# Weight matrices stored as column blocks in a one-core hybrid diffusion layer: each row of a load 4 KB long instead of eight pieces of 512 bytes

## The reference

```python
hx = modulate(rms_norm(x, norm1_w), sh1, sc1)            # shifts and scales from c @ w_mod
hc = modulate(rms_norm(ctx, norm1_w), csh1, csc1)
rx, rgx, qx, kx, vx, gax, gbx = split_cols(hx @ w_in)    # w_in: 1024 x 5632
rc, _, _, kc, vc, _, _        = split_cols(hc @ w_in)
# (A) RG-LRU in both directions over conv(rx), started from the context's last states
y_r = (h_f + h_b) * gelu(rgx)
# (B) windowed attention, 8 heads of 128, 2 key heads, window 128, context keys, a sink per head
y_a = windowed_attention(rope(qx), rope(kx), vx, kc, vc, sink)
y = sigmoid(gax) * (y_r @ w_o_rnn) + sigmoid(gbx) * (y_a @ w_o_attn)
x = x + g1 * (y @ w_out)
hx2 = modulate(rms_norm(x, norm2_w), sh2, sc2)
a, v = split(dwconv(hx2 @ w_up, 3 taps))                 # w_up: 1024 x 6144
x = x + g2 * ((gelu(a) * v) @ w_down)                    # w_down: 3072 x 1024
return rms_norm(x, final_norm_w)
```

## Time and profile before

| | us |
|---|---|
| median of 3 runs | 1898.85 |
| lowest, highest | 1897.75, 1898.92 |
| the profiled execution | 1898.04 |
| its span | 1896.3 |
| busy in the span: TensorE | 1776.7 |
| VectorE | 1223.6 |
| ScalarE | 714.8 |
| GpSimd | 591.6 |

### The profile page before, as it was taken

One profiled execution on the slowest core, in us unless ns is written; L12 is line 12 of the kernel. 1 busy time (PEld: TensorE's weight loads), 2 busy tenths in 40 slices (PEclk: granted clock), 3 DMA queues, 4 the chain that ended last, 5 costly groups with the idle time before them and its releaser, 6 DMA issues.

```text
span 1896.3 us, 23019 instructions
## 1 busy us (share of the span) xinstructions
PE 1776.7 (94%) x8276; PEld 1466.8 (77%) x8276; DVE 1223.6 (65%) x1355; ACT 714.8 (38%) x919; POOL 591.6 (31%) x276
## 2 busy tenths in 40 slices
PE   3998899999899979999998798999999999999997
PEld 1887688888688768878886675888888888888886
DVE  5873667768513777775114679999998988525423
ACT  5433666557200157771002014544444444302202
POOL 2125777676344745534452680000000000000000
PEclk8999899999899979999999899999999999999999
DMA  9124112111245300005223661232222223622212
GB/s 365 49 89 122 42 48 67 59 58 45 87 135 177 77 12 1 0 27 170 81 66 135 236 199 39 89 96 81 88 77 88 77 88 119 230 100 85 99 44 90
DMA packets 184525, 182.11 MB, mean 96 GB/s; under 512 B 10512, under 2 KB 162448, under 8 KB 182288
## 3 DMA queue, kind: packets, MB, share of 16 engines
q1 hardware_dynamic: 176784, 148.26, 24.3%
q10 hardware_dynamic: 7680, 33.04, 5.2%
HBM read 145.09 MB, written 30.93 MB: 93 GB/s over the span
## 4 chain that ended last, share of the span: by engine, by line
PE 69%; DVE 16%; DMA 4%; issue 4%; ACT 3%; POOL 3%; ACTq 1%; SPq 0%; DVEq 0%; POOLq 0%
PE acc L840 14%; PE acc L841 13%; PE acc L842 13%; PE gp L840 9%; PE gp L842 9%; PE gp L841 9%; DVE pt_lo L2095 2%; DVE smax L2065 2%; DMA wst<-in_w_out 2%; DMA qs<-qf 1%; DVE wgr L2131 1%; DVE yq L2048 1%; POOL wlo_both L687 1%; PE acc L875 1%; POOL whi_both L685 1%
## 5 line engine op out<-in xcount | busy, mean ns | idle before, releaser
L840 PE MATMUL acc<-hx_hi,whi_both 128*128 128x512 f32 x672 | 265.6, 395 | 43.2 <-POOL wlo_both L687 23.0
L841 PE MATMUL acc<-hx_lo,whi_both 128*128 128x512 f32 x672 | 264.6, 394 | 0.0
L842 PE MATMUL acc<-hx_hi,wlo_both 128*128 128x512 f32 x672 | 263.9, 393 | 0.0
L685 POOL TENSOR_TENSOR whi_both<-wst,ones 128x1024 fp32r<-128x1024 f32 x63 | 169.1, 2683 | 286.0 <-PE acc L842 203.2
L687 POOL TENSOR_TENSOR wlo_both<-wst,whi_both 128x1024 fp32r<-128x1024 f32 x63 | 189.0, 2999 | 4.9
L840 PEld LDWEIGHTS acc<-hx_hi,whi_both 128*128 128x128 f32 x672 | 128.1, 191 | 71.8 <-POOL wlo_both L687 23.7
L842 PEld LDWEIGHTS acc<-hx_hi,wlo_both 128*128 128x128 f32 x672 | 128.0, 190 | 27.2
L841 PEld LDWEIGHTS acc<-hx_lo,whi_both 128*128 128x128 f32 x672 | 128.2, 191 | 25.9
L840 PE MATMUL acc<-T_hi,fac_hi 128*128 128x512 f32 x264 | 102.8, 389 | 0.3 <-DVE fac_lo L2289 0.3
L842 PE MATMUL acc<-T_hi,fac_lo 128*128 128x512 f32 x264 | 102.7, 389 | 0.0
L841 PE MATMUL acc<-T_lo,fac_hi 128*128 128x512 f32 x264 | 102.7, 389 | 0.0
(11 more groups left out here) (335 smaller groups left out, 4782.6 us busy)
## 6 DMA issues: line engine op xcount, KB each, us to landing
wst<-in_w_in SPq DMA_DIRECT2D x50, 512.0 KB, 3.9
wst<-in_w_up SPq DMA_DIRECT2D x26, 512.0 KB, 4.6
wgr<-in_mod_rest ACTq DMA_DIRECT2D x6, 2048.0 KB, 10.5
ffn_row_scratch<-ca SPq DMA_DIRECT2D x24, 512.0 KB, 2.6
wst<-in_w_down SPq DMA_DIRECT2D x32, 384.0 KB, 3.3
g_in<-ffn_row_scratch SPq DMA_DIRECT2D x24, 512.0 KB, 6.4
wup<-in_w_up SPq DMA_DIRECT2D x22, 512.0 KB, 4.9
wmod<-in_mod_first SPq DMA_DIRECT2D x8, 1024.0 KB, 11.6
```

The lines of the kernel that those rows point to most:

```text
L685: nc.gpsimd.tensor_tensor(whi[s][:, 0:kc, :], wst[s][:, 0:kc, :], ones_of(kc), mult).then_inc(S["w_hi"], 1)
L840: mm(out_ap, w_h, x_h, start=first, stop=False)
L841: mm(out_ap, w_h, x_l, start=False, stop=False)
L842: return mm(out_ap, w_l, x_h, start=False, stop=last)
```

## The change

Each weight matrix is given to the kernel in another order. The host copies the matrix into blocks of 128 columns, and within a block puts first the partition, then the eight chunks of rows, then the columns. A block is then 512 KB in one piece, and the 4 KB that belong to a partition are contiguous. `w_down` is cut also into its four pieces of 768 rows, so a row of a load is 3 KB. In the kernel only the source address patterns change; a block is now picked by its number. Sizes, order, queues and waits of the loads stay. Each of SP's loads `wst<-in_w_in 128x8x128` becomes `wst<-in_w_in 128x1024`, and in loops six register instructions on SP ahead of other loads and stores are no longer emitted.

```diff
-            w_in = D["w_in"][0].rearrange("(k p) n -> p k n", p=P)
-            w_or = D["w_o_rnn"][0].rearrange("(k p) n -> p k n", p=P)
-            w_oa = D["w_o_attn"][0].rearrange("(k p) n -> p k n", p=P)
-            w_out = D["w_out"][0].rearrange("(k p) n -> p k n", p=P)
-            w_up = D["w_up"][0].rearrange("(k p) n -> p k n", p=P)
-            w_dn = D["w_down"][0].rearrange("(k p) n -> p k n", p=P)
+            w_in, w_or, w_oa, w_out, w_up = (D[n] for n in ("w_in", "w_o_rnn", "w_o_attn", "w_out", "w_up"))
+            w_dn = D["w_down"]
 
             def col(w, base, i):
-                return w[:, :, ds(base + i * P, P)] if not isinstance(i, int) else w[:, :, base + i * P:base + i * P + P]
+                if isinstance(i, int):
+                    return w[base // P + i]
+                return w.rearrange("b p k n -> p b k n")[:, ds(i + base // P, 1), :, :].rearrange("p o k n -> p (o k) n")
...
-                sp.dma_start(wst[n % 2][:, 0:PK, :], w_dn[:, PK * q:PK * (q + 1), P * m:P * (m + 1)]).then_inc(dn_loaded[n % 2], 16)
+                sp.dma_start(wst[n % 2][:, 0:PK, :], w_dn[q, m]).then_inc(dn_loaded[n % 2], 16)
...
+def by_column_block(w):
+
+    w = np.asarray(w)[0]
+    return np.ascontiguousarray(w.reshape(KC, P, -1, P).transpose(2, 1, 0, 3))
+
+
+def by_piece(w):
+
+    return np.ascontiguousarray(np.asarray(w)[0].reshape(PIECES, PK, P, KC, P).transpose(0, 3, 2, 1, 4))
...
+    arrays.update({n: by_column_block(inputs[n]) for n in ("w_in", "w_o_rnn", "w_o_attn", "w_out", "w_up")})
+    arrays["w_down"] = by_piece(inputs["w_down"])
```

## The result

| | before | changed |
|---|---|---|
| median of 6 runs each, us | 1897.41 | 1882.55 |
| lowest, highest | 1896.27, 1898.92 | 1877.26, 1886.70 |
| the profiled execution | 1898.04 | 1886.70 |
| its span | 1896.3 | 1884.9 |
| its mean granted clock | 0.973 | 0.976 |

The ratio is 0.9925, with a 95% interval from 0.9905 to 0.9945: 14.9 us less by the medians, 17.9 were predicted, and the range 1872 to 1890 holds it. But no execution took 1882.55 us. Three took 1877.3 to 1879.5, three 1885.6 to 1886.7, and the median is the middle between the two groups. The profiled execution is of the upper one, and there the gain is 11.3 us.

The account below looks back on a forecast made before the run. TensorE, busy 94% of the span, was taken as the bound nearly everywhere. Terms 1.6 + 6.3 + 10.0 = 17.9 us off 1898.04 gave 1880.1, plus 0.8 for the median of runs: 1881.0 us, range 1872 to 1890.

Parts of the forecast that it names:

- Stage of w_out, -10.0: Stage of `w_out`: block 1 lands with the first `wgr` group, TensorE restarts at 1045.1; 10.0 us less, floor 5, ceiling 18.
- equal turns by packets: Stage of `w_out`: each of 16 engines takes one packet from each queue in turn, so block 1 needs 8 turns, not 64.
- no new wait: Stage of `w_out`: block 2 lands at about 1051 and is split by 1057, so TensorE gets no new wait.
- Rival (d): Stage of `w_out`: VectorE becomes the bound, its sums slowed beside GpSimd; stage +5.1 us, total 1903.5 us; chance 0.03.
- Rival (c): Stage of `w_out`: block 1 is through ahead of the first group and the clock stays up; 1872.9 us; chance 0.12.
- Before attention, -6.3: Query stage before attention: both long swaps of query halves shorten; 6.3 us less, floor 0, ceiling 6.8.
- Without that both swaps take 2.31 us: Before attention: once the weight load no longer holds them, the 6.07 and 5.34 us swaps shorten, saving 3.76 + 3.03 = 6.8.
- rival (b): Before attention: the swaps stay long, held by `kff` and `vf`, giving 0 there; 1887.2 us; chance 0.14.
- Context stage, -1.6: Context stage: faster `w_in` loads shorten TensorE's waits at round ends; 1.6 us less, floor 0.5, ceiling 3.8.
- Two loads stand on the chain: 2 x 0.8: Context stage: two `w_in` loads of about 4 us lie on the chain of waits, each gaining 0.8 us.
- A load alone, -0.8: Any 512 KB weight load in flight alone: 4 KB rows save 0.5 to 1.4 us, taken as 0.8.
- Elsewhere 0: Start and other stages: no gain, since work on x or the matmuls of the block before cover the loads.

Follow-up runs that it names:

- 2 KB rows: Changed kernel with `w_out` stored so a load has 256 rows of 2 KB instead of 128 of 4 KB; 1881.7 us, one execution.
- the added wait: GpSimd waits for VectorE's rotation before splitting in the query stage; in the kernel before 1888.4 us (0.9954), in the changed kernel 1877.2 us (0.9897).
- the three variants without the added wait: Kernel before with only `w_out` relaid, 1887.0 us; block 1 of `w_out` sent early, 1890.7; `kff` and `vf` loaded after query blocks 2 and 3, 1897.2.
- `kff` and `vf` behind: Loads of `kff` and `vf` moved behind query blocks 2 and 3 on SP's queue; changed kernel 1878.1 us, kernel before 1897.2 us (1.0017).
- ScalarE's high parts: Changed kernel with high parts of `w_out` blocks 1 to 7 made by ScalarE instead of GpSimd; 1876.9 us, ratio 0.9920.
- The kernel of all changes together: Changed kernel plus `kff` and `vf` after query blocks 2 and 3, high parts on ScalarE, block 1 of `w_out` sent early; 1872.8 us, 0.9878.
- the early block: Kernel before, short rows kept, block 1 of `w_out` sent ahead of SP's wait for the merged rows; 1890.7 us, ratio 0.9963.

## Why the prediction was right, and where it was wrong

**Stage of w_out, -10.0: right, 10.6 measured.** Block 1 landed after 11.2 us (10 to 14 expected), the restart came at 1044.2 (1045.1), the clock still fell, and and with `w_out` alone relaid the stage is shorter by 10.5 us. Its mechanism, equal turns by packets, stands for this stage: 42 and 44 packets, and 2 KB rows land in between. The 10.7 us between the last residuals (1134.06 and 1123.38) have three parts. TensorE restarts 11.4 us earlier (1055.61 and 1044.20). Product 1, from its first matmul to that of product 2, takes 13.35 us (to 1057.55), 13.0 before, since the lower clock lasts 5 us of it and not 4.3: that gives back 0.4. And a new wait of 0.3 us stands ahead of product 6, which the prediction's "no new wait" had left out. It comes from VectorE. VectorE was expected ready at 1058 to 1060 and took the residual of product 1 at 1058.18, about 0.4 us after it could have, following eight sums of which four were over 2 us. It worked on to 1106.9 without a pause, and the chain of waits of the changed kernel now runs through its sums, a late residual, the load of block 6 and its split:

```profile
1081.95 1.21 DVE yq L2190
...
1084.02 10.47 DMA wst<-in_w_out
...
1097.97 3.26 POOL wlo_both L685
...
1101.28 0.50 PE acc L838
```

So VectorE has nothing to spare, and the 0.5 us taken off for it was about right (0.3). Rival (d) has begun in its mechanism, but at 0.3 us and not 5.1. Rival (c) did not come: block 1 passed the first group, but by 1.5 us, and the clock was lost.

The Trainium skill, "DMA: Bandwidth & Descriptors", section "Queues, rings and completion order", has an engine drain 9 to 17 descriptors of a queue before it switches. Block 1's time depends on the number of its rows, 11.2, 14.4 and 22.9 us, which bundles of 9 to 17 pieces would not give, so here an engine changed queue after each of them.

The turns are not the whole of it. In the query stage a queue that started beside a long backlog of SP's got no turn at first. The store of `t_scratch`, sent on ScalarE's queue at 572.3 in the kernel before, moved its first packets at about 577, and from 578 to 580 the two queues were equal again (94 and 90 packets). The first swap, sent from 582.63 on in the changed kernel, moved its first at about 585.4, while the third, sent beside an almost empty queue, began within about 1 us. What holds a new queue back for 3 to 5 us isn't shown.

**Before attention, -6.3: the step is wrong.** Both swaps stay long in a long execution (5.74 and 4.70 us), the last copy starts at 667.12, and the term is 0. In a short one an execution ends 7 to 9 us earlier than a long one of the same kernel, more than the ceiling of 6.8 that I set, but the kernel before has short ones too. The step that failed is "Without that both swaps take 2.31 us", with the sentence that the rounds of 10.82 us never work lateness off. I read 10.82 from the chain and did not ask what it is made of. The row `yq<-yq,qs` had 3.24 us on VectorE in that round, where the same instruction takes 1.23 alone: the lateness is kept by GpSimd, and the length of the second swap follows from it, since a late swap meets the next load. With the added wait the rounds do work the lateness off. The first swap did lose its short neighbours, but 4 KB rows of the same load, `kff` and `vf` still stand ahead of it (from 584 to 585 us the 16 engines moved 116 packets of SP's queue, 0.42 MB, and none of the swap), and it took 7.6 us from its first send instead of 8.0.

What the rows change is the odds. With `w_in` in short pieces 16 of 71 executions of the kernel before were short, and 5 of 36 of the three variants without the added wait; with it in long rows 7 of 12 of the changed kernel, and 17 of 24 of three variants of it (all but `w_out`; `kff` and `vf` behind; ScalarE's high parts). The kernel of all changes together isn't counted, since its six executions do not fall in two clear groups. The odds differ between sessions (6 of 29, 8 of 17, 2 of 12 and 0 of 7 for the kernel before), so the comparison within one session is the safer one: 8 of 12 with all but `w_out` relaid against 6 of 29 beside it. That `w_in` is the matrix that does it is argued from the place of the race; it was not relaid alone. Half a microsecond ahead of that add is worth 8 us or nothing.

So rival (b), 1887.2 us with 0.14, is what 5 of 12 executions did (1884.4 to 1886.7), though not because `kff` and `vf` hold the swap: moved behind, they changed nothing with short rows. The other seven took 1876.6 to 1879.5. The forecast of 1881.0 is close to the mean of the twelve, 1881.2, and no execution is there. That the median of the first six, 1882.55, came so near is luck: 10.6 us of the gain are the forecast's, the rest is how many executions of each kind happened to fall into either sample.

**Context stage, -1.6: wrong, 0.1 in the profiled execution and some 0.7 in others.** From the first context copy to GpSimd's split for the next stage took 24.6 us before and 24.5 changed; in the other profiles it is 24.7 to 24.8 with `w_in` in short pieces (four) and 24.0 to 24.3 with long rows (eight). The step is "Two loads stand on the chain: 2 x 0.8", and the floor of 0.5 was none. Loads do land sooner there, 3.2 us instead of 3.9 as the median from 140 to 160 us, but behind the load ScalarE has its copy of the product before, which waits for TensorE. ScalarE's timeline of the changed kernel:

```profile
151.23 0.56 ACT L1246 ACTIVATE xc_ctx<-gp,pcol 128x256 f32<-128x256 f32 x1 [2.27 <-PE gp L840]
151.74 1.06 ACT L1246 ACTIVATE whi_both<-wst 128x1024 fp32r<-128x1024 f32 x1
```

The high part starts right behind that copy: the load is there, and this round is set by product, copy, high part, low part. (In the round before it, at 147.90, the high part still waited 0.55 us for its load, the one of 4.29 us.) From the copy at 143.89 to this one are 7.3 us; it was 7.5. A shorter step in a loop uncovers the next one.

**A load alone, -0.8: right.** The median falls by 0.7 us in that stretch, though the one load on the chain needs 4.29. The Trainium skill, "DMA: Bandwidth & Descriptors", section "Specifications", has 512 bytes as enough for full rate; the 3.9 and 3.2 us disagree with it, but the difference earned little here.

**Elsewhere 0: nearly right.** In the profiled execution the kernel is 0.1 us ahead at the start of the stage of `w_out`, 10.7 at its end and 11.4 at the end of the span, so 0.7 came behind it; where, was not looked into. Packets under 2 KB fell to 10896, as forecast.

## What to carry to other kernels

Where two queues feed the same DMA engines and both are moving, count packets and not bytes: a load in many small rows waits for as many packets of the other queue as it has rows, and a longer row or an earlier send frees it alike. Before subtracting from a round of a loop, take it apart: if it is as long as another engine's step, something may lock them, and a row that takes 3.23 us where it takes 1.23 elsewhere shows what. When executions fall in groups, the median may be a time that none has; take a profile of each group, and ask whether a change moved a level or the odds. Here it did both.

## What the runs showed that was not expected

- The kernel before has two outcomes, 1888.1 and 1897.4 us by the medians of 16 and 55 executions, from one race, decided by 1 us or less, between VectorE's add and GpSimd's split. None of the first six executions showed it. One semaphore wait more, on the engine that is early, makes it 9 us faster at the median.
- An engine that is early can cost: the early block let GpSimd split beside VectorE's last merge steps (3.41 and 2.14 us for 1.2), which gave back 3.1 us.
- With the turns taken one row at a time, the same 512 KB in 8, 16 and 64 rows per engine landed after 11.2, 14.4 and 22.9 us.
